# Part of a branch's normalisation moved from VectorE to GpSimd, and the additions put one step earlier

## The reference

```python
def rmsnorm(x, g):
    xf = x.astype(jnp.float32)
    y = xf * lax.rsqrt(jnp.mean(xf * xf, axis=-1, keepdims=True) + RMS_EPS)
    return (y * g.astype(jnp.float32)).astype(x.dtype)

def first_block(x, ...):
        h = rmsnorm(x, norm_mix_pre[l])
        ...                                                   # projections, RG-LRU, windowed attention -> mix
        x = x + rmsnorm(mix @ w_out[l], norm_mix_post[l])     # norm 1, first branch addition
        h = rmsnorm(x, norm_mlp_pre[l])                       # norm 2
        u = jnp.square(jax.nn.relu(h @ w_mlp_up[l]))
        x = x + rmsnorm(u @ w_mlp_down[l], norm_mlp_post[l])  # norm 3, second branch addition
```

## Time and profile before

| | us |
|---|---|
| median of 3 runs | 2830.33 (2827.31 to 2831.86) |
| the profiled execution | 2830.53 |
| its span | 2828.7 |
| PE busy | 2759.5 (98%) |
| DVE busy | 1949.4 (69%) |
| ACT busy | 1337.7 (47%) |
| POOL busy | 109.7 (4%) |

### The profile page before, as it was taken

One profiled execution on the slowest core, in us unless ns is written; L12 is line 12 of the kernel. 1 busy time (PEld: TensorE's weight loads), 2 busy tenths in 40 slices (PEclk: granted clock), 3 DMA queues, 4 the chain that ended last, 5 costly groups with the idle time before them and its releaser, 6 DMA issues.

```text
span 2828.7 us, 50381 instructions
## 1 busy us (share of the span) xinstructions
PE 2759.5 (98%) x16433; PEld 2408.3 (85%) x16433; DVE 1949.4 (69%) x3013; ACT 1337.7 (47%) x2135; POOL 109.7 (4%) x206
## 2 busy tenths in 40 slices
PE   7999999999999999999999999999999999999998
PEld 6888888888887888888888789788888888888887
DVE  7878867766657775457755654855788885688855
ACT  5655555554444443334444444644554444444443
POOL 0000000000010000000000010100110000000000
PEclk9999999999999999999999999999999999999999
DMA  4454544444553556666654454354445555555554
GB/s 177 173 178 178 183 162 149 150 176 178 188 192 128 187 184 223 212 200 206 213 193 184 157 185 152 139 174 145 161 164 184 187 173 196 196 183 188 184 174 162
DMA packets 83197, 503.33 MB, mean 178 GB/s; under 512 B 9686, under 2 KB 17926, under 8 KB 31516
## 3 DMA queue, kind: packets, MB, share of 16 engines
q1 hardware_dynamic: 79868, 491.04, 49.4%
q0 software_dynamic: 3120, 11.14, 1.5%
q10 hardware_dynamic: 144, 0.30, 0.0%
HBM read 500.29 MB, written 10.55 MB: 181 GB/s over the span
## 4 chain that ended last, share of the span: by engine, by line
PE 59%; DVE 5%; issue 3%; ACT 2%; DVEq 0%; ACTq 0%
PE PS L568 33%; PE PS L572 17%; ACT w L1128 1%; PE PS L688 1%; PE PS L689 1%; PE PS L690 1%; PE PS L583 1%; DVE tmp L1716 1%; DVE w L1705 1%; PE PS L585 1%; PE PS L584 1%; DVE tmp L2149 0%; DVE tmp L2148 0%; PE PS L878 0%; PE PS L600 0%
## 5 line engine op out<-in xcount | busy, mean ns | idle before, releaser
L1705 DVE TENSOR_TENSOR w<-w_raw,w 128x1024 fp32r<-128x1024 f32 (+1 forms) x964 | 1099.9, 1173 | 422.5 <-ACT w L1128 420.9
L1128 ACT ACTIVATE w<-w_raw 128x1024 fp32r<-128x1024 f32 (+1 forms) x964 | 941.8, 1010 | 388.0 <-PE PS L572 232.3
L568 PE MATMUL PS<-h,w 128*128 128x512 f32 x3008 | 768.1, 397 | 6.0 <-ACT gates L1240 1.8
L568 PEld LDWEIGHTS PS<-h,w 128*128 128x128 f32 x3008 | 540.8, 189 | 121.7 <-issue 17.4
L568 PE MATMUL PS<-u,w 128*128 128x512 f32 x1728 | 442.1, 394 | 5.2 <-ACT w L1128 5.2
L572 PEld LDWEIGHTS PS<-h,w 128*128 128x128 f32 x3008 | 410.8, 190 | 30.3
L572 PE MATMUL PS<-h,w 128*128 128x256 f32 x3008 | 419.3, 282 | 0.0
L568 PEld LDWEIGHTS PS<-u,w 128*128 128x128 f32 x1728 | 309.0, 190 | 58.5 <-ACT w L1128 5.8
L568 PE MATMUL PS<-f,w 128*128 128x512 f32 x1408 | 354.1, 393 | 4.0 <-DVE x L2390 4.0
L568 PEld LDWEIGHTS PS<-f,w 128*128 128x128 f32 x1408 | 254.0, 189 | 49.7 <-DVE x L2390 4.2
L572 PEld LDWEIGHTS PS<-u,w 128*128 128x128 f32 x1728 | 241.4, 190 | 21.1
(11 more groups left out here) (326 smaller groups left out, 2608.6 us busy)
## 6 DMA issues: line engine op xcount, KB each, us to landing
w_raw<-in_w_FU SPq DMA_DIRECT2D x88, 1024.0 KB, 4.7
w_raw<-in_w_UP SPq DMA_DIRECT2D x64, 1024.0 KB, 4.8
w_raw<-in_w_DN SPq DMA_DIRECT2D x64, 1024.0 KB, 4.8
w_raw<-in_w_FD SPq DMA_DIRECT2D x64, 704.0 KB, 4.1
w_raw<-in_w_G SPq DMA_DIRECT2D x32, 1024.0 KB, 4.7
w_raw<-in_w_Q SPq DMA_DIRECT2D x18, 1024.0 KB, 4.7
w_raw<-in_w_X SPq DMA_DIRECT2D x16, 1024.0 KB, 4.8
w_raw<-in_w_Y SPq DMA_DIRECT2D x16, 1024.0 KB, 4.7
```

The costliest lines, as they stand in the source:

```text
L568: pe.matmul(PS[:, bank, :], w_hi[:, 2 * s + hf, k * P:(k + 1) * P], rhs[:, k0 + k].rearrange("p a b -> p (a b)"), start=start and k == 0, ...
L1128: act.activation(w_hi[:, 2 * s + hf, 0:n * P], w_raw[:, s, off * P:(off + n) * P], ACT.Copy)\
L1705: tt(w_lo[:, slot, 0:n * P], w_raw[:, s, off * P:(off + n) * P], w_hi[:, slot, 0:n * P].bitcast(F32), ALU.subtract).then_inc(lo_ready, 1)
```

## The change

GpSimd gets a function `scale_branch`. After norm 1's factor is ready it multiplies the pairs 1, 2, 4, 5, 6 and 7 of `qy`, after norm 3's the pairs 1, 3, 5 and 7; VectorE multiplies the others. The reciprocal now raises a semaphore `rstd_ready`, on which both engines wait, and GpSimd's products raise `branch_scaled_2`. At the first place VectorE adds pair p + 1 before it forms the low parts of pair p (it did so after them). VectorE's two loops are written out.

```diff
--- before.py
+++ after.py
@@ -43,6 +43,7 @@
 SC = 384
 JOB_C, JOB_A, JOB_B = 0, 12, 16
 N_CMP = S // 16 - 1
+POOL_PAIRS = {1: (1, 2, 4, 5, 6, 7), 3: (1, 3, 5, 7)}
 CMP_LEN = 32
 KV_C = 3
 
@@ -255,8 +256,10 @@
         hv_ready = sem("hv_ready")
         h_hi_ready = sem("h_hi_ready")
         h_ready = sem("h_ready")
+        rstd_ready = sem("rstd_ready")
         gain_scaled = sem("gain_scaled")
         branch_scaled = sem("branch_scaled")
+        branch_scaled_2 = sem("branch_scaled_2")
         x_new = sem("x_new")
 
         rows_mm = sem("rows_mm")
@@ -460,9 +463,18 @@
                 pool.wait_ge(s1_ready, t)
                 pool.tensor_copy(q1s[:], qy[:, t, :]).then_inc(q1_staged, 1)
 
+            def scale_branch(norm, pairs):
+                pool.wait_ge(rstd_ready, norm + 1)
+                pool.wait_ge(gain_scaled, NC_D * (norm + 1) // 2)
+                for p in pairs:
+                    own = slice(2 * p, 2 * p + 2)
+                    pool.tensor_tensor(qy[:, own, :], qy[:, own, :], windows(tmp[3], 0, P, 0, [[0, 2], [1, S]]), ALU.mult)\
+                        .then_inc(branch_scaled_2, 1)
+
             for norm in range(1, 5):
                 if norm % 2:
                     add_squares(norm)
+                    scale_branch(norm, POOL_PAIRS[norm])
                 else:
                     free_last_square(norm)
                 if norm == 2:
@@ -1715,14 +1727,14 @@
 
                 return dve.tensor_reduce(out, PS[:, s, :].rearrange("p (a b) -> p b a", a=2), AX.X, ALU.add)
 
-            n_norm, n_h, n_b = [0], [0], [0]
+            n_norm, n_h, n_b, n_ours, n_theirs = [0], [0], [0], [0], [0]
             rstd = tmp[3][:, 0:S]
 
             def inverse_deviation(out=rstd):
                 n_norm[0] += 1
                 dve.wait_ge(std_ready, n_norm[0])
-                link(dve.reciprocal(out, tmp[2][:, 0:S]))
-                link.flush()
+                dve.reciprocal(out, tmp[2][:, 0:S]).then_inc(rstd_ready, 1)
+                dve.wait_ge(rstd_ready, n_norm[0])
 
             rstd_twice = windows(tmp[3], 0, P, 0, [[0, 2], [1, S]])
 
@@ -1770,14 +1782,22 @@
 
                 inverse_deviation()
 
+                theirs = POOL_PAIRS[n_norm[0] - 1]
+                ours = [p for p in range(NC_D // 2) if p not in theirs]
+
                 def scaled(p):
+                    if p in theirs or p >= NC_D // 2:
+                        return
                     dve.wait_ge(gain_scaled, n_b[0] + 2 * p + 2)
-                    own = bass.ds(2 * p, 2)
-                    tt(qy[:, own, :], qy[:, own, :], rstd_twice, ALU.mult).then_inc(branch_scaled, 2)
+                    own = slice(2 * p, 2 * p + 2)
+                    tt(qy[:, own, :], qy[:, own, :], rstd_twice, ALU.mult).then_inc(branch_scaled, 1)
 
                 def add(p):
-                    dve.wait_ge(branch_scaled, n_b[0] + 2 * p + 2)
-                    own = bass.ds(2 * p, 2)
+                    if p in theirs:
+                        dve.wait_ge(branch_scaled_2, n_theirs[0] + theirs.index(p) + 1)
+                    else:
+                        dve.wait_ge(branch_scaled, n_ours[0] + ours.index(p) + 1)
+                    own = slice(2 * p, 2 * p + 2)
                     tt(x[:, own, :], x[:, own, :], qy[:, own, :], ALU.add).then_inc(x_new, 2)
 
                 def lo(p):
@@ -1788,17 +1808,18 @@
                 scaled(0)
                 if next_gain:
                     add(0)
-                    with dve.Fori(0, NC_D // 2 - 1) as p:
+                    for p in range(NC_D // 2 - 1):
                         scaled(p + 1)
+                        add(p + 1)
                         lo(p)
-                        add(p + 1)
                     lo(NC_D // 2 - 1)
                     n_h[0] += NC_D
                 else:
-                    with dve.Fori(0, NC_D // 2 - 1) as p:
+                    for p in range(NC_D // 2):
                         scaled(p + 1)
                         add(p)
-                    add(NC_D // 2 - 1)
+                n_ours[0] += len(ours)
+                n_theirs[0] += len(theirs)
                 n_b[0] += NC_D
 
             def first_lo():
```

## The result

The changed kernel is slower: 2836.41 us (median of 9 runs, 2833.59 to 2840.42) against 2829.67 us, a ratio of 1.0027 with a 95% interval of 1.0018 to 1.0036 (the two medians by themselves give 1.0024). The medians are 6.7 us apart. The profiled execution's span grew from 2828.7 to 2834.6 us.

What follows compares the result with a forecast made beforehand. TensorE was taken as the bound, busy nearly throughout, so savings count only where it waits. Delays of 5.5 and 4.2 us plus 1.0 us of clock gave 10.7 us, hence a median of 2841.0 us, range 2834 to 2847.

Steps and rivals of the forecast that it cites:

- the second case: Rival at both places: GpSimd holds the port for one operation, VectorE takes turns; 7.3 us slower, 2837.6 us; chance 0.25.
- the first case: Main case at both places: GpSimd keeps the port through its whole row of products; 10.7 us slower, 2841.0 us; chance 0.60.
- the products and VectorE stop each other: Both places: with two SBUF inputs on VectorE, each 512-element GpSimd product stops it for 1.12 us, or 1.00 us.
- How long the product takes: GpSimd's 128x512 product at both places: 1.24 to 1.36 us, 1.2 us from one to the next.
- Who gets the port: Both places: GpSimd's six or four products in a row keep VectorE out, as three earlier copies without waits did.
- Place 1: Behind norm 1: six products delay VectorE's first addition 7.0 us and TensorE's low run 5.5 us.
- Place 2: Behind norm 3: four products delay the first addition and everything behind the last square by 4.2 us.
- TensorE's clock: Both places: TensorE idles some 5 us, so a half-clock stretch at each; 1.0 us together (0 to 5).
- if nothing else happened: Gain from VectorE's fewer products: 0.9 us at the first place, 0.4 us at the second, 1.3 us in all.
- The unrolling at nothing: VectorE's two loops written out: no effect, since their register work ran under the 0.68 us operations.
- The other sign: Rival at both places: products do not stop VectorE; 2829.0 us, no change that can be measured; chance 0.10.

Runs made afterwards that it cites:

- E4: Changed kernel with GpSimd writing zeros to its pairs and reading nothing, in place of multiplying; ratio to the kernel before 0.9999 (0.9990 to 1.0008).
- E5: Changed kernel with GpSimd's products raising one semaphore after the last, not one each; profiled execution 2841.6 us.
- E6: Changed kernel with each GpSimd product split into two of 256 elements, semaphore on the second; profiled execution 2833.4 us.
- E9: Changed kernel with four GpSimd copies of 128x128 in place of each product, signal behind the last; profiled execution 2829.8 us.
- E12: Changed kernel with strided GpSimd copies for each product, at the first place also one on 15 partitions; profiled execution 2827.4 us.
- E3: Changed kernel with no product on GpSimd, only the written-out loops and new order left; ratio to the kernel before 1.0011 (1.0002 to 1.0020).
- E10: Changed kernel with GpSimd multiplying only pairs 6 and 7 at the first place, starting after VectorE's sixth addition; profiled execution 2829.8 us.
- E7: Changed kernel with GpSimd multiplying pair 7 only, at both places; profiled execution 2832.2 us.
- E2: Changed kernel with GpSimd multiplying its four pairs at the second place only; ratio to the kernel before 1.0013 (1.0004 to 1.0022).

## Why the prediction was right, and where not

The sign was right, and so was its ground, that the two engines stop each other. How they share the port was wrong in the forecast, and the time, 2841.0 us, was 4.6 us too high. The measured 2836.4 us lies in the range because the range was drawn down to 2834 to take in the second case; the first case by itself was reckoned at 2838 us or more. Point by point:

- That the products and VectorE stop each other, for a 512-element product by 1.12 us (1.00 to 1.12): right. The longest addition took 1.76 us for 0.69 us, 1.07 us more, and E4 shows the cause.
- How long the product takes, 1.24 to 1.36 us and 1.2 us from one to the next: right, 1.26 us alone (E5).
- "Who gets the port": the step that failed. I let GpSimd keep the port through all six, by rows 7. VectorE's first addition should have started 7.0 us late; it was issued on time and took 0.9 us longer. VectorE gets in behind one product, whether it signals (changed kernel), does not (E5, E6) or is a copy (E9, E12). What happened is my second case, with 0.25. The rule that I had from the Trainium skill, "SBUF — State Buffer", taken instruction by instruction, was the one that held (first additions of 1.57 and 1.58 us; the section "Who interferes with whom" words it for two-port modes, the page's summary for two SBUF inputs as well). I had set one group of rows with three copies above it, and that place went the other way in the changed kernel's trace.
- Place 1, 5.5 us in the forecast, 3.8 us in the second case, 4.7 us measured. The fourth pair of low parts ended 870.31 - 854.58 = 15.73 us after the reciprocal's start, where it was 867.33 - 854.99 = 12.34 us, so 3.4 us later. That is six stops of about 1.0 us, less the three products (pairs 1, 2 and 4) that VectorE no longer makes ahead of it and the 0.3 us of the order (12.03 us in E3). The other 1.3 us came between there and the low run. It is put down to TensorE's clock, at half from 867.4 to 870.8 with TensorE busy throughout; E6, with the clock at 1.00, hasn't got it.
- Place 2, 4.2 us, in the second case 3.0 us, measured 3.7 us. The third pair of squares started 9.38 us after the reciprocal, before 6.60 us (1601.83 - 1595.23): 2.8 us; the remaining 0.9 us came behind it, where the half-clock stretch lies.
- TensorE's clock, 1.0 us in the forecast, 0.5 us in the second case: too small for the two places, 2.2 us together. One half-clock stretch at each, as said. But the stretch of rows 9, behind the second place, was gone, and in the last 1200 us the changed execution was 1.7 us shorter (1206.85 for 1208.58 us from the low products of C2 to the end), where the trace before has a stretch at half the clock at 1994.9 and the other has none. The sum of the trace: 4.7 + 3.7 - 0.4 (ahead of place 1) - 0.3 (between) - 0.15 (from the reciprocal behind place 2 to C2's low products) - 1.7 = 5.9 us, the growth of the span. I had no term for what falls elsewhere, and it goes both ways from run to run. It is luck that it makes the second case's 2837.6 us look so close: the two places cost 8.4 us, where that case has 7.3 us with its clock, and 2.5 us came back elsewhere.
- The gain "if nothing else happened", 0.9 and 0.4 us: E4 shows both, 0.86 and 0.48 us. The unrolling at nothing: right at the second place (0.07 us, E3). The new order had no term: with the unrolling it shortened the first place by 0.6 us (E3).
- The other sign, products that do not stop VectorE, 2829.0 us and no change that can be measured: it did not happen. E4 puts instructions that don't stop VectorE in their place, and its median of 2828.7 us can't be told from the kernel before.

## What to carry to other kernels

Work moved from VectorE to GpSimd is not taken off VectorE when both read SBUF and VectorE's instructions have two SBUF inputs: a product of 0.60 us was exchanged for a stop of 1.07 us. It can pay where VectorE stands idle, or where GpSimd merely writes (E4), and perhaps where one of VectorE's inputs is in PSUM. That no experiment tried, but the trace before has VectorE reading PSUM with a copy of GpSimd beside it, 14 times like this:

```profile
376.36 0.96 DVE L2021 SCALAR_TENSOR_TENSOR sb<-PS,mask 128x768 f32<-128x768 f32 x1 [0.60 <-PE PS L774]
376.40 0.40 POOL L461 COPY q1s<-qy 128x256 f32 x1 [12.06 <-PE PS L774]
```

The copy ran inside VectorE's instruction and took 0.40 us, as a copy of this size takes with VectorE idle (line 508, 1725.69 us). Find the stop first in instructions of both engines that already run side by side in the trace. If work must go to GpSimd, cut it into short instructions (E6) and let it start behind VectorE's first, awaited operations (E10); neither made the kernel faster here.

## What the runs showed of the hardware that I had not expected

- In every row of products and copies that I tried, VectorE and GpSimd took turns, instruction by instruction. GpSimd with a row of instructions ready didn't keep the port; the exception is the place of the earlier trace rows, where it ran its copies unbroken in 11 of 14 traces, for a reason that is open. VectorE waits for one instruction, up to 1.07 us for 512 elements with two inputs, 0.5 us for 256, 0.1 us for a copy of 128.
- Behind one delay of 1.1 us at the head of a chain of small TensorE operations came 3.3 us at half the clock (E7), and the place cost 2.0 us. With the same times on VectorE, a stretch that began 1.4 us sooner and lasted 6.8 us in place of 3.4 us made a place 0.7 us longer (E2 against the changed kernel). How VectorE's stops and the stretches hang together was not varied on its own.
